# The entry half of the feed-forward layers: x rewritten in place as the normalized input, and 2 columns fewer per matmul

## The chip, the cores and the metric

The kernel runs on one core of a Trainium2 chip. The metric is the device time of one execution in microseconds (us). The engines are named as in the profile: PE is the matmul engine (TensorE), PEld its loading of weights, DVE is VectorE, ACT is ScalarE, POOL is GpSimd, SP is SyncE, which issues most of the DMAs.

## The reference

Two layers of an encoder are run over 576 tokens (512 of a prompt and 64 of a sample, which have different modulation vectors). Each layer has two feed-forward blocks around a mixer:

```
h += 1/2 * gate1 * RMSNorm(SwiGLU(mod1(RMSNorm(h))))
x  = mod2(RMSNorm(h)); ... ; h += gate2 * RMSNorm(m @ W_out)
h += 1/2 * gate3 * RMSNorm(SwiGLU(mod3(RMSNorm(h))))

def pre_mod(h, g_pre, shift, scale):
    return rmsnorm(h, g_pre) * (1 + scale[:, None, :]) + shift[:, None, :]
def swiglu(x, w1, w2):
    g, u = jnp.split(x @ w1, 2, axis=-1)
    return (jax.nn.silu(g) * u) @ w2
```

The model width is 1024, the inner width of the feed-forward blocks is 2752, and all values are fp32.

## The kernel before

**Tiling.** Activations lie transposed, with 128 features on the partitions and the 576 tokens along the free axis, so x is 8 tiles (KD) of 128x576. A weight chunk is 128x1024: the 8 tiles that take all of x to one block of 128 outputs. The first matrix of a feed-forward block has 43 chunks, which alternate between g (even) and u (odd), and chunk 42 holds the remaining 64 + 64 outputs. There are four such phases: "f1a" and "f1b" of layer 0 and of layer 1. They are called here 0a, 0b, 1a and 1b.

**Three products for one.** Every operand is split into a high and a low fp32r part, and `split_tile` (the matmul at L769) makes hi\*hi, lo\*hi and hi\*lo, each in two halves of the tokens (b = 0 and 1). A tile is thus 6 matmuls and a chunk 48. The weights are split on the way: SP loads a chunk into `w_raw` (5 slots), ACT casts it to `w_hi` (`split_hi`, L1296), DVE subtracts to get `w_lo` (`split_lo`, L1715), and PE waits in `chunk_ready` for the `w_lo` of a chunk. Both engines take the chunks strictly in order, wherever `split_hi()` and `split_lo()` stand in their programs. When a phase begins, chunks 0 to 4 are through or on their way; in `ffn_up` the next calls make chunks 5, 6, 7, and so on.

**The norm after the matmul.** `x_hi`/`x_lo` hold h\*(1+scale)\*gain, without the factor r2 = 1/rms and without the shift. Two extra moving columns (`moving(1)`, 290 columns in place of 288) carry the shift vectors of prompt and sample through the same weights. DVE then reads each chunk's result with `take` (L1792, L1793): it multiplies by `r2` and copies the two shift sums to `c_col`; the shift is added as the bias of the Silu on ACT (L1323) and in the product of g and u on DVE (L1765). ACT casts the product to `hid_hi` (L1327) and DVE makes `hid_lo` (L1770) for the second matrix.

**Order.** The result of a chunk lies in one of four pairs of PSUM banks. Chunks 0, 1 and 2 use pairs 0, 1 and 2 and are taken without r2 by ACT (`first_raw`, L1344), as r2 is being made meanwhile. Then even chunks use pair 0 and odd ones pair 1, one after the other (`whole_chunk`), each waiting in `pair_free` until the chunk before it in its pair was taken. On ACT and DVE `ffn_up` is a loop over i, the block of chunks 2i and 2i+1. Between these steps DVE works through "ada" units (L1729, two passes and two reads of the accumulator each), parts of the modulation vectors for later stages, out of two slots that POOL refills (L2432); their results pass through banks 5 and 6, which belong to pairs 2 and 3. `f1_units` says how many units stand in block i: 3 in most.

Of the kernel before, what the change touches and what calls it, by code (L numbers as in the profile page):

```python
# [8 lines left out]
ACT = mybir.ActivationFunctionType  # L9
# [65 lines left out]
          ("f1b", F1_CHUNKS), ("f2b", KF)]  # L75
TRI_PAIRS = [0, 1, 2] + [(g + T + 1) % 2 for T in range(1, NP + 1) for g in range(3)]
GROUPS = [("f1a", KF - 1, KF - 1), ("f2a", KD // 2, KD // 2), ("tri", TRI_PAIRS.count(0), TRI_PAIRS.count(1)), ("uc", 1, 1),
          ("gate", 3 * KD, 3 * KD), ("out", 4, 3), ("f1b", KF - 1, KF - 1), ("f2b", KD // 2, KD // 2)]
# [75 lines left out]
def chunk(l, ph, i):  # L154
    return l * CHUNK_N + CHUNK_AT[ph][0] + i
# [216 lines left out]
def build_program(nc, ins, outs):  # L372
# [64 lines left out]

    rms = sb("rms", [P, 3, TOK], at=big + 2 * TOK * 4)
# [122 lines left out]
    hid_ready = S("hid_ready", 2 * KF)  # L561
# [29 lines left out]
    sil_ready = S("sil_ready", 2 * KF)  # L591
    g_scaled = S("g_scaled", 4)
# [164 lines left out]
    def _(pe):  # L757
# [1922 lines left out]
```

## Time and profile before

| | |
|---|---|
| median of 3 runs | 2693.69 us (2693.58 to 2693.96) |
| the profiled execution | 2693.93 us, of which the span is 2691.9 us |
| PE | busy 2658.2 us, 99% of the span, 20698 matmuls |
| DVE | busy 1635.2 us, 61% |
| ACT | busy 962.4 us, 36% |
| POOL | busy 199.4 us, 7% |

The span reaches from the first to the last instruction of the profiled execution, and its own time has 2 us more around it. Rows of a time line give the start, the duration and the number of instructions merged into one row, and in brackets the idle time of the engine just before and what ended it. The duration of a matmul holds its pipeline, so it is longer than the distance to the next one.

### The profile page before, as it was taken

How to read it: one execution, taken by the hardware profiler on the slowest of the kernel's cores; microseconds unless marked ns; L12 is line 12 of the kernel's file. 1: busy time of each engine (PE TensorE's matmuls, PEld its weight loads, DVE VectorE, ACT ScalarE, POOL GpSimd, SP SyncE). 2: the span in 40 equal slices, each digit the busy share in tenths (PEclk: the TensorE clock that was granted, in tenths of full speed). 3: DMA queues.
4: the chain of work that ended last, by engine and by line, in shares of the span. 5: the costliest groups of instructions: out<-in, count | busy, mean ns of one | idle time of the engine just before them, and what ended most of it. 6: DMA issues, size and time to landing. Idle time of an engine off the chain costs nothing.

```text
span 2691.9 us, 49072 instructions
## 1 busy us (share of the span) xinstructions
PE 2658.2 (99%) x20698; PEld 2575.7 (96%) x20698; DVE 1635.2 (61%) x3542; ACT 962.4 (36%) x1792; POOL 199.4 (7%) x371
## 2 busy tenths in 40 slices
PE   7999999999999999999999999999999999999997
PEld 6999999888999999999999999998889999999997
DVE  4677666765655577776577776276655445555523
ACT  4222324444422442232252222255452236322321
POOL 0111110110000001111101111001100000000000
PEclk9999999999999999999999999999999999999999
DMA  6344453343333224445424445234332222333321
GB/s 260 126 145 139 158 177 112 123 130 107 95 111 109 87 95 153 135 144 163 136 88 152 137 159 157 88 101 141 119 104 81 85 83 75 98 108 104 95 81 65
DMA packets 92987, 324.79 MB, mean 121 GB/s; under 512 B 13980, under 2 KB 17628, under 8 KB 92064
## 3 DMA queue, kind: packets, MB, share of 16 engines
q1 hardware_dynamic: 62512, 221.72, 25.9%
q0 software_dynamic: 30256, 99.93, 11.2%
q8 instruction: 164, 2.69, 0.4%
q14 instruction: 55, 0.45, 0.0%
HBM read 310.70 MB, written 11.55 MB: 120 GB/s over the span
## 4 chain that ended last, share of the span: by engine, by line
PE 97%; DVE 1%; DMA 0%; issue 0%; ACT 0%; DVEq 0%; SPq 0%; ACTq 0%
PE ps L769 90%; PE ps L1131 2%; PE ps L1179 1%; PE ps L1155 1%; PE ps L778 1%; DMA ada_first<-in_ada_first 0%; PE ps L1148 0%; PE ps L823 0%; DVE prob L2242 0%; PE ps L909 0%; PE ps L1192 0%; DVE next L1792 0%; PE ps L807 0%; PE ps L832 0%; PE ps L1055 0%
## 5 line engine op out<-in xcount | busy, mean ns | idle before, releaser
L769 PE MATMUL ps<-x_hi,w_hi 128*128 128x288 f32 (+1 forms) x4224 | 940.1, 298 | 2.4 <-DVE x_lo L1883 1.5
L769 PE MATMUL ps<-x_lo,w_hi 128*128 128x288 f32 (+1 forms) x4224 | 934.2, 297 | 0.0
L769 PE MATMUL ps<-x_hi,w_lo 128*128 128x288 f32 (+1 forms) x4224 | 927.1, 295 | 0.0
L769 PEld LDWEIGHTS ps<-x_hi,w_hi 128*128 128x128 f32 x4224 | 685.2, 189 | 14.2 <-issue 8.0
L769 PEld LDWEIGHTS ps<-x_hi,w_lo 128*128 128x128 f32 x4224 | 688.3, 189 | 0.0
L769 PEld LDWEIGHTS ps<-x_lo,w_hi 128*128 128x128 f32 x4224 | 687.8, 189 | 0.3
L1715 DVE TENSOR_TENSOR w_lo<-w_raw,w_hi 128x1024 fp32r<-128x1024 f32 x384 | 467.7, 1222 | 158.8 <-ACT w_hi L1296 156.7
L1296 ACT CAST w_hi<-w_raw 128x1024 fp32r<-128x1024 f32 x384 | 391.5, 1048 | 69.4 <-DMA w_raw<-in_f 68.7
L769 PE MATMUL ps<-hid_hi,w_hi 128*128 128x288 f32 x1344 | 301.3, 295 | 0.0
L769 PE MATMUL ps<-hid_hi,w_lo 128*128 128x288 f32 x1344 | 299.8, 294 | 0.0
L769 PE MATMUL ps<-hid_lo,w_hi 128*128 128x288 f32 x1344 | 299.8, 294 | 0.0
L1729 DVE CUSTOM_DVE_ANT_0 ps<-ada_w,c_half,ada_all 128x512 f32<-128x512 f32 x256 | 193.5, 756 | 113.9 <-DMA ada_w<-in_ada 113.5
L2432 POOL DMA_DIRECT2D ada_w<-in_ada x256 | 137.7, 538 | 1639.2 <-DVE ada_all L1729 1634.9
L769 PEld LDWEIGHTS ps<-hid_hi,w_hi 128*128 128x128 f32 x1344 | 220.0, 188 | 0.2
L769 PEld LDWEIGHTS ps<-hid_lo,w_hi 128*128 128x128 f32 x1344 | 219.6, 188 | 0.2
L1327 ACT CAST hid_hi<-hid 128x576 fp32r<-128x576 f32 x84 | 56.6, 674 | 453.5 <-DVE hid L1765 453.5
L769 PEld LDWEIGHTS ps<-hid_hi,w_lo 128*128 128x128 f32 x1344 | 217.5, 188 | 0.0
L1729 DVE CUSTOM_DVE_ANT_0 ada_w<-ada_w,c_half,ada_all 128x512 f32<-128x512 f32 x256 | 191.3, 747 | 0.0
L1323 ACT ACTIVATE sil<-sil,z 128x512 f32<-128x512 f32 (+1 forms) x168 | 80.9, 529 | 249.8 <-DVE z L1793 249.6
L1792 DVE TENSOR_TENSOR hid<-ps,r 128x576 f32<-128x576 f32 x80 | 60.6, 757 | 152.9 <-PE ps L769 152.9
L1808 DVE TENSOR_TENSOR acc_y<-acc_y,sq 128x576 f32<-128x576 f32 (+1 forms) x51 | 32.9, 645 | 177.2 <-ACT sq L1367 151.4
L1367 ACT ACTIVATE sq<-ps 128x576 f32<-128x576 f32 x38 | 24.8, 654 | 299.0 <-PE ps L778 266.0
(243 smaller groups left out, 2440.9 us busy)
## 6 DMA issues: line engine op xcount, KB each, us to landing
w_raw<-in_f SPq DMA_DIRECT2D x260, 512.0 KB, 3.7
ada_w<-in_ada POOLq DMA_DIRECT2D x256, 256.0 KB, 4.0
w_raw<-in_gate SPq DMA_DIRECT2D x64, 512.0 KB, 3.7
w_raw<-in_tri SPq DMA_DIRECT2D x40, 512.0 KB, 3.7
ada_first<-in_ada_first SPq DMA_DIRECT2D x4, 2048.0 KB, 20.6
w_raw<-in_wout SPq DMA_DIRECT2D x16, 512.0 KB, 3.6
c_half<-c_scratch POOLq DMA_DIRECT2D x11, 512.0 KB, 5.8
decay_p<-f_prompt POOLq DMA_DIRECT2D x8, 512.0 KB, 4.4
```

Source lines behind the costliest of these rows:

```text
L769: r = mm(ps[:, 2 * out + b, 0:width], w, xx[:, cols(b)], start=first and n == 0, stop=last and n == 2)
L778: r = mm(ps[:, 2 * out + b, 0:HALF], w[:, s, t * P:(t + 1) * P], hid_hi[:, k, columns(b)], start=False, stop=w is w_lo)
L1131: r = mm(out, q_st[rows, i * P:i * P + m], k, start=True, stop=True)
L1155: r = turn_in(out, prob[0:m, place(u), b * P:b * P + w], const[0:m, IDENT, 0:m])
L1296: copy(w_hi[:, c % SLOTS, :], w_in[:, c % SLOTS, :]).then_inc(hi_ready.sem, 1)
L1323: r = A(sil[:, i, part], sil[:, i, part], ACT.Silu, bias=c_col[:, 2 * (i % 2), g:g + 1])
L1327: copy(hid_hi[:, i, :], hid[:, i, :]).then_inc(prod_hi.sem, 1)
L1715: V.tensor_tensor(w_lo[:, s, :], w_in[:, s, :], w_hi[:, s, :], ALU.subtract).then_inc(lo_ready.sem, 1)
L1729: r = V.tensor_tensor_reduce(out, ada_w[:, u % 2, :], c_half[:, g, :], 1.0, so_far, ALU.mult, ALU.add, so_far)
L1792: V.tensor_tensor(two(dst), pair[p], two(r2[:, :]), ALU.mult)
L1808: V.tensor_tensor(total, total, more, ALU.add).then_inc(y_added.sem, 1)
L2432: nc.gpsimd.dma_start(dst, src).then_inc(signal.sem, 16)
```

## The change

In all four first-matrix phases, chunks 0 to 5 stay as they are. Chunks 6 and 7 are run together, tile by tile, into pairs 2 and 3 (`chunk_pair`), and still read the old x. After block 1, DVE makes h\*r2 in four steps of two tiles (`h_times_r2`) and ACT turns each tile into the full normalized and shifted input `x_full` (`full_of_h`, two ACTIVATEs each). When chunks 6 and 7 have read tile k of the old x, ACT overwrites `x_hi` of this tile (`high_of_full`) and DVE `x_lo` (`low_of_full`). Chunks 8 and 9 are again run together, into pairs 0 and 1, each tile after its `x_full_ready`, and from there on all matmuls have 288 columns. From block 4 on, ACT applies the Silu straight from PSUM and DVE multiplies u from PSUM with it: there is no scaling by r2, no shift and no copy of shift sums. The ada units move to blocks 5 to 10 and 12 to 17, up to 4 in each.

```diff
@@ -73,9 +73,11 @@
 assert 2 * TAIL == P
 CHUNKS = [("f1a", F1_CHUNKS), ("f2a", KF), ("tri", 3 * (NP + 1)), ("uc", 2), ("gate", 4 * KD), ("out", KD),
           ("f1b", F1_CHUNKS), ("f2b", KF)]
+NORMED = 4
+F1_GROUPS = KF - 2
 TRI_PAIRS = [0, 1, 2] + [(g + T + 1) % 2 for T in range(1, NP + 1) for g in range(3)]
-GROUPS = [("f1a", KF - 1, KF - 1), ("f2a", KD // 2, KD // 2), ("tri", TRI_PAIRS.count(0), TRI_PAIRS.count(1)), ("uc", 1, 1),
-          ("gate", 3 * KD, 3 * KD), ("out", 4, 3), ("f1b", KF - 1, KF - 1), ("f2b", KD // 2, KD // 2)]
+GROUPS = [("f1a", F1_GROUPS, F1_GROUPS), ("f2a", KD // 2, KD // 2), ("tri", TRI_PAIRS.count(0), TRI_PAIRS.count(1)), ("uc", 1, 1),
+          ("gate", 3 * KD, 3 * KD), ("out", 4, 3), ("f1b", F1_GROUPS, F1_GROUPS), ("f2b", KD // 2, KD // 2)]
 
 N_MODS = DEPTH * N_MOD
 
@@ -123,7 +125,13 @@
 
 def f1_units(l, ab, i):
 
-    return 0 if i in (2, 11, KF - 2) else 1 if (l, ab) == (1, "b") else 3
+    n = 2 if (l, ab) == (1, "b") else 4
+    return n if 5 <= i < 11 or 12 <= i < 18 else 0
+
+
+def f1_group(p, i):
+
+    return i - 2 + p if i >= NORMED else i // 2 if p == 0 else i
 
 
 def f2_units(l, ab):
@@ -435,6 +443,7 @@
     sil = sb("sil", [P, KF, TOK], at=big)
     hid = sb("hid", [P, KF - 1, TOK], at=big + KF * TOK * 4)
 
+    x_full = sb("x_full", [P, KD, TOK], at=big + 6 * TOK * 4)
     rms = sb("rms", [P, 3, TOK], at=big + 2 * TOK * 4)
     sq_h = sb("sq_h", [P, KD, TOK], at=big + 5 * TOK * 4)
 
...
+    sil_ready = S("sil_ready", 2 * (NORMED + 1))
+    g_scaled = S("g_scaled", 6)
     tail_made = S("tail_made", 2)
     tail_in = S("tail_in", 2, step=32)
     q_scaled = S("q_scaled", NP)
...
@@ -798,6 +812,22 @@
                 r = split_tile(p, c, t, hi[:, t, :], lo[:, t, :], cols, t == 0, t == KD - 1)
             r.then_inc(chunk_done.sem, 1)
 
+        def chunk_pair(l, ph, i, pairs, cols, ab):
+
+            c = chunk(l, ph, 2 * i)
+            chunk_ready(c)
+            chunk_ready(c + 1)
+            for k in range(KD):
+                n = (ab == "b") * KD + k
+                if i == NORMED:
+                    pe.wait_ge(x_full_ready.sem, x_full_ready.done(l, n))
+                for s in (0, 1):
+                    r = split_tile(pairs[s], c + s, k, x_hi[:, k, :], x_lo[:, k, :], cols, k == 0, k == KD - 1)
+                    if k == KD - 1:
+                        r.then_inc(chunk_done.sem, 1)
+                if i < NORMED and k < KD - 1:
+                    r.then_inc(x_read.sem, 1)
+
         def x_half(l, ph, s, k, b):
 
             return split_tile(s, chunk(l, ph, s), k, x_hi[:, k, :], x_lo[:, k, :], moving, k == 0, k == KD - 1, (b,))
@@ -925,13 +955,18 @@
             whole_chunk(l, ph, 3, 1, 1, x_hi, x_lo, moving,
                         gate=(lambda t: t == BANDS_AT and sum_of_h(*((l, n - 1) if n else (l - 1, 2))))
                         if l or n else None)
-            for i in range(2, KF):
-                whole_chunk(l, ph, 2 * i, 0, i - 1, x_hi, x_lo, moving)
+            whole_chunk(l, ph, 4, 0, f1_group(0, 2), x_hi, x_lo, moving)
+            whole_chunk(l, ph, 5, 1, f1_group(1, 2), x_hi, x_lo, moving)
+            if l or n:
+                pe.wait_ge(norm_made.sem, norm_made.done(*((l, n - 1) if n else (l - 1, 2))))
+            chunk_pair(l, ph, 3, (2, 3), moving, ab)
+            for p in (0, 1):
+                pair_free(l, ph, p, f1_group(p, NORMED))
+            chunk_pair(l, ph, NORMED, (0, 1), split_columns, ab)
+            for i in range(NORMED + 1, KF):
+                whole_chunk(l, ph, 2 * i, 0, f1_group(0, i), x_hi, x_lo, split_columns)
                 if i < KF - 1:
-                    whole_chunk(l, ph, 2 * i + 1, 1, i, x_hi, x_lo, moving)
-                if i == 2 and (l or n):
-
-                    pe.wait_ge(norm_made.sem, norm_made.done(*((l, n - 1) if n else (l - 1, 2))))
+                    whole_chunk(l, ph, 2 * i + 1, 1, f1_group(1, i), x_hi, x_lo, split_columns)
             ph = "f2" + ab
             at = 0 if ab == "a" else KF + KD
             for o in range(KD - 1):
...
-            for i in range(KF - 1):
+            for i in range(NORMED):
                 if i == 1 and not l and ab == "a":
                     split_hi()
                 if i < 2:
-                    act.wait_ge(g_scaled.sem, g_scaled.done(l, (ab == "b") * 2 + i))
+                    act.wait_ge(g_scaled.sem, g_scaled.done(l, first + i))
+                elif i == 2:
+                    split_hi()
+                    act.wait_ge(acc_free[0].sem, acc_free[0].done(l, GROUP_AT[ph][0] + f1_group(0, i)))
                 else:
-                    split_hi()
-                    act.wait_ge(acc_free[0].sem, acc_free[0].done(l, GROUP_AT[ph][0] + i - 1))
+                    for k in range(KD):
+                        high_of_full(l, ab, k)
+                        if k in (2, 5):
+                            split_hi()
+                    act.wait_ge(g_scaled.sem, g_scaled.done(l, first + 2))
                 for g, part in ((0, slice(0, SEQ)), (1, slice(SEQ, TOK))):
                     r = A(sil[:, i, part], sil[:, i, part], ACT.Silu, bias=c_col[:, 2 * (i % 2), g:g + 1])
                 r.then_inc(sil_ready.sem, 1)
 
                 act.wait_ge(hid_ready.sem, hid_ready.done(l, mine + i))
                 copy(hid_hi[:, i, :], hid[:, i, :]).then_inc(prod_hi.sem, 1)
-                if i > 1:
+                if i == 1:
+                    for k in range(KD):
+                        full_of_h(l, ab, k)
+                if i == 2:
                     split_hi()
+            for i in range(NORMED, KF - 1):
+                split_hi()
+                act.wait_ge(chunk_done.sem, chunk_done.done(0, chunk(l, ph, 2 * i)))
+                A(two(sil[:, i, :]), pair[0], ACT.Silu).then_inc(acc_free[0].sem, 1)
+                split_hi()
+                act.wait_ge(acc_free[1].sem, acc_free[1].done(l, GROUP_AT[ph][1] + f1_group(1, i)))
+                copy(hid_hi[:, i, :], hid[:, i, :]).then_inc(prod_hi.sem, 1)
             split_hi()
             act.wait_ge(tail_in.sem, tail_in.done(l, ab == "b"))
             A(tail_gu[0:TAIL, :], tail_gu[0:TAIL, :], ACT.Silu)
             A(tail_ug[TAIL:P, :], tail_ug[TAIL:P, :], ACT.Silu).then_inc(sil_ready.sem, 1)
-            act.wait_ge(hid_ready.sem, hid_ready.done(l, mine + KF - 1))
+            act.wait_ge(hid_ready.sem, hid_ready.done(l, mine + NORMED))
             copy(hid_hi[:, KF - 1, :], tail_hid[:, :]).then_inc(prod_hi.sem, 1)
+
+        def full_of_h(l, ab, k):
+
+            n = 0 if ab == "a" else 2
+            act.wait_ge(x_times_r2.sem, x_times_r2.done(l, (n // 2 * KD + k) // 2))
+            for g, part in ((0, slice(0, SEQ)), (1, slice(SEQ, TOK))):
+                r = A(x_full[:, k, part], x_full[:, k, part], ACT.Identity, scale=pre_scale[:, n, k, g:g + 1],
+                      bias=shifts(l, n)[:, k, g:g + 1])
+            r.then_inc(x_full_made.sem, 1)
+
+        def high_of_full(l, ab, k):
+
+            n = (ab == "b") * KD + k
+            act.wait_ge(x_full_made.sem, x_full_made.done(l, n))
+            if k < KD - 1:
+                act.wait_ge(x_read.sem, x_read.done(l, (ab == "b") * (KD - 1) + k))
+            else:
+                chunk_over(l, "f1" + ab, 7)
+            copy(halves_of(x_hi[:, k, :]), two(x_full[:, k, :])).then_inc(x_full_high.sem, 1)
 
         def first_raw(l, ab):
 
...
@@ -1752,13 +1822,21 @@
                     take(hid[:, 1, :], 1, 3).then_inc(acc_free[1].sem, 1)
                 elif i == 1:
                     split_lo()
+                    h_times_r2(0)
+                elif i == 2:
+                    dve.wait_ge(chunk_done.sem, chunk_done.done(0, chunk(l, ph, 4)))
+                    take(sil[:, i, :], 0, 0).then_inc(acc_free[0].sem, 1)
+                    split_lo()
+                    dve.wait_ge(chunk_done.sem, chunk_done.done(0, chunk(l, ph, 5)))
+                    take(hid[:, i, :], 1, 1).then_inc(acc_free[1].sem, 1)
                 else:
-                    dve.wait_ge(chunk_done.sem, chunk_done.done(0, chunk(l, ph, 2 * i)))
-                    take(sil[:, i, :], 0, 2 * (i % 2)).then_inc(acc_free[0].sem, 1)
-                    split_lo()
-                    ada(l, ph, f1_units(l, ab, i) // 2)
-                    dve.wait_ge(chunk_done.sem, chunk_done.done(0, chunk(l, ph, 2 * i + 1)))
-                    take(hid[:, i, :], 1, 2 * (i % 2) + 1).then_inc(acc_free[1].sem, 1)
+                    for k in range(KD):
+                        low_of_full(l, ab, k)
+                        if k in (2, 5):
+                            split_lo()
+                    dve.wait_ge(chunk_done.sem, chunk_done.done(0, chunk(l, ph, 7)))
+                    take(sil[:, i, :], 2, 2).then_inc(g_scaled.sem, 1)
+                    take(hid[:, i, :], 3, 3)
                 dve.drain()
                 dve.wait_ge(sil_ready.sem, sil_ready.done(l, mine + i))
                 for g, part in ((0, slice(0, SEQ)), (1, slice(SEQ, TOK))):
...
@@ -1766,26 +1844,48 @@
                                                scalar=c_col[:, 2 * (i % 2) + 1, g:g + 1], in1=sil[:, i, part],
                                                op0=ALU.add, op1=ALU.mult)
                 r.then_inc(hid_ready.sem, 1)
+                if i == 1:
+                    for k in range(2, KD, 2):
+                        h_times_r2(k)
                 dve.wait_ge(prod_hi.sem, prod_hi.done(l, at + i))
                 V.tensor_tensor(hid_lo[:, i, :], hid[:, i, :], hid_hi[:, i, :], ALU.subtract
                                 ).then_inc(prod_lo.sem, 1)
-                if i > 1:
+                if i == 2:
                     split_lo()
-                    ada(l, ph, f1_units(l, ab, i) - f1_units(l, ab, i) // 2)
+            for i in range(NORMED, KF - 1):
+                split_lo()
+                ada(l, ph, f1_units(l, ab, i) // 2)
+                dve.wait_ge(chunk_done.sem, chunk_done.done(0, chunk(l, ph, 2 * i + 1)))
+                dve.wait_ge(acc_free[0].sem, acc_free[0].done(l, GROUP_AT[ph][0] + f1_group(0, i)))
+                V.tensor_tensor(two(hid[:, i, :]), pair[1], two(sil[:, i, :]), ALU.mult).then_inc(acc_free[1].sem, 1)
+                split_lo()
+                dve.wait_ge(prod_hi.sem, prod_hi.done(l, at + i))
+                V.tensor_tensor(hid_lo[:, i, :], hid[:, i, :], hid_hi[:, i, :], ALU.subtract
+                                ).then_inc(prod_lo.sem, 1)
+                ada(l, ph, f1_units(l, ab, i) - f1_units(l, ab, i) // 2)
             i = KF - 1
...
             upper = hid_hi[TAIL:P, i, :]
             V.tensor_tensor(upper, tail_hid[TAIL:P, :], upper, ALU.subtract).then_inc(prod_lo.sem, 1)
+
+        def h_times_r2(k):
+
+            V.tensor_tensor(x_full[:, k:k + 2, :], h[:, k:k + 2, :], r2[:, :].rearrange("p (a n) -> p a n", a=1)
+                            .to_broadcast((P, 2, TOK)), ALU.mult).then_inc(x_times_r2.sem, 1)
+
+        def low_of_full(l, ab, k):
+
+            dve.wait_ge(x_full_high.sem, x_full_high.done(l, (ab == "b") * KD + k))
+            V.tensor_tensor(halves_of(x_lo[:, k, :]), two(x_full[:, k, :]), halves_of(x_hi[:, k, :]), ALU.subtract
+                            ).then_inc(x_full_ready.sem, 1)
 
         def take(dst, p, c):
 
```

Left out are the declarations of the changed semaphores, and the tail (chunk 42), where two small additions of the shift go. New are the semaphores `x_read`, `x_times_r2`, `x_full_made`, `x_full_high` and `x_full_ready`.

## Rows read from the trace of the kernel before

**Rows 1.** The page: its head, busy time by engine.
```profile
span 2691.9 us, 49072 instructions
...
PE 2658.2 (99%) x20698; PEld 2575.7 (96%) x20698; DVE 1635.2 (61%) x3542; ACT 962.4 (36%) x1792; POOL 199.4 (7%) x371
```

**Rows 2.** The page: the chain that ended last, shares by line.
```profile
PE ps L769 90%; PE ps L1131 2%; PE ps L1179 1%; PE ps L1155 1%; PE ps L778 1%; DMA ada_first<-in_ada_first 0%; PE ps L1148 0%; PE ps L823 0%; DVE prob L2242 0%; PE ps L909 0%; PE ps L1192 0%; DVE next L1792 0%; PE ps L807 0%; PE ps L832 0%; PE ps L1055 0%
```

**Rows 3.** The chain in order of time, phase 1b and after.
```profile
2282.21 270.14 PE ps L769 x2034
...
2570.02 16.59 PE ps L769 x126
...
2655.59 8.29 PE ps L769 x63
```

**Rows 4.** Time line of all engines, pair 1 being freed in 0a.
```profile
49.93 0.65 ACT L1344 COPY hid<-ps 128x576 f32<-128x576 f32 x1
...
50.72 0.37 PE L769 MATMUL ps<-x_hi,w_hi 128*128 128x288 f32 x1 [0.48 <-ACT hid L1344]
```

**Rows 5.** DVE time line, phase 1b.
```profile
2292.77 1.22 DVE L1715 TENSOR_TENSOR w_lo<-w_raw,w_hi 128x1024 fp32r<-128x1024 f32 x1
2294.08 0.95 DVE L1765 SCALAR_TENSOR_TENSOR hid<-hid,z,sil 128x512 f32<-128x512 f32 x2
...
2297.18 1.21 DVE L1715 TENSOR_TENSOR w_lo<-w_raw,w_hi 128x1024 fp32r<-128x1024 f32 x1
2299.77 0.76 DVE L1792 TENSOR_TENSOR hid<-ps,r 128x576 f32<-128x576 f32 x1 [1.38 <-PE ps L769]
...
2325.26 0.76 DVE L1792 TENSOR_TENSOR hid<-ps,r 128x576 f32<-128x576 f32 x1 [4.42 <-PE ps L769]
```

**Rows 6.** ACT time line, phase 1b.
```profile
2291.97 0.96 ACT L1323 ACTIVATE sil<-sil,z 128x512 f32<-128x512 f32 x2
2295.06 0.67 ACT L1327 CAST hid_hi<-hid 128x576 fp32r<-128x576 f32 x1 [2.13 <-DVE hid L1765]
2295.64 1.05 ACT L1296 CAST w_hi<-w_raw 128x1024 fp32r<-128x1024 f32 x1
```

**Rows 7.** DVE time line, phase 0a.
```profile
60.91 1.23 DVE L1715 TENSOR_TENSOR w_lo<-w_raw,w_hi 128x1024 fp32r<-128x1024 f32 x1 [0.19 <-ACT w_hi L1296]
...
70.11 0.76 DVE L1792 TENSOR_TENSOR hid<-ps,r 128x576 f32<-128x576 f32 x1 [3.57 <-PE ps L769]
```

**Rows 8.** Groups by line and shape, ACT.
```profile
L1371 ACT ACTIVATE z<-ps,z 128x288 f32<-128x288 f32 x48 | 23.7, 495 | 0.0
...
L1308 ACT ACT_TABLE_LOAD x3 | 3.8, 1283 | 0.1
```

**Rows 9.** Groups by line and shape, PE.
```profile
L823 PE MATMUL ps<-sq_h,const 128*32 128x288 f32 x160 | 11.8, 412 | 0.0
...
L892 PE MATMUL ps<-sq_in,const 128*32 128x288 f32 x32 | 4.1, 687 | 11.6 <-DVE sq_in L2002 11.6
```

**Rows 10.** Stretches: length, busy PE, PEld, DVE, ACT, POOL, clock, DMA share, GB/s.
```profile
20.00:23.50 3.50, 1.56 (x9) 1.13 (x9) 3.50 (x6) 3.43 (x7) 0.00 (x0) 1.00 1.01 418
23.50:24.00 0.50, 0.50 (x5) 0.50 (x4) 0.50 (x2) 0.50 (x1) 0.00 (x0) 0.85 1.01 426
24.00:24.50 0.50, 0.50 (x7) 0.22 (x9) 0.46 (x2) 0.01 (x1) 0.00 (x0) 0.50 1.06 451
27.00:27.50 0.50, 0.50 (x20) 0.44 (x12) 0.00 (x0) 0.00 (x0) 0.00 (x0) 0.73 1.00 426
```

**Rows 11.** DVE time line, ada units in 0a.
```profile
114.40 0.09 DVE L1729 DVE_READ_ACCUMULATOR2_ANT ada_all<- 128x1 f32 x1
...
118.95 0.76 DVE L1729 CUSTOM_DVE_ANT_0 ps<-ada_w,c_half,ada_all 128x512 f32<-128x512 f32 x1 [1.25 <-DMA ada_w<-in_ada]
...
121.10 0.76 DVE L1792 TENSOR_TENSOR hid<-ps,r 128x576 f32<-128x576 f32 x1 [0.72 <-PE ps L769]
```

More of the change, by code:

```diff
@@ L560, in build_program @@
     prod_lo = S("prod_lo", 2 * KF + KD)
-    hid_ready = S("hid_ready", 2 * KF)
+    hid_ready = S("hid_ready", 2 * (NORMED + 1))
+    x_read = S("x_read", 2 * (KD - 1))
+    x_times_r2 = S("x_times_r2", KD)
+    x_full_made = S("x_full_made", 2 * KD)
+    x_full_high = S("x_full_high", 2 * KD)
+    x_full_ready = S("x_full_ready", 2 * KD)
     merged = S("merged", KD)
@@ L1302, in ffn_up @@
             ph, at = "f1" + ab, (0 if ab == "a" else KF + KD)
-            mine = 0 if ab == "a" else KF
+            mine, first = (0, 0) if ab == "a" else (NORMED + 1, 3)
             if l or ab == "b":
@@ L1738, in ffn_up @@
             ph, at = "f1" + ab, (0 if ab == "a" else KF + KD)
-            mine = 0 if ab == "a" else KF
+            mine, first = (0, 0) if ab == "a" else (NORMED + 1, 3)
             if l or ab == "b":
                 norm_of_h(*((l, 1) if ab == "b" else (l - 1, 2)))
-            for i in range(KF - 1):
+            for i in range(NORMED):
                 if i == 0:
@@ L1771, in ffn_up @@
                                 ).then_inc(prod_lo.sem, 1)
-                if i > 1:
+                if i == 2:
                     split_lo()
-                    ada(l, ph, f1_units(l, ab, i) - f1_units(l, ab, i) // 2)
+            for i in range(NORMED, KF - 1):
[9 more added lines that the diff above has]
+                ada(l, ph, f1_units(l, ab, i) - f1_units(l, ab, i) // 2)
             i = KF - 1
             dve.wait_ge(chunk_done.sem, chunk_done.done(0, chunk(l, ph, 2 * i)))
-            take(tail_gu[:, :], 0, 2 * (i % 2)).then_inc(acc_free[0].sem, 1)
+            V.tensor_copy(two(tail_gu[:, :]), pair[0]).then_inc(acc_free[0].sem, 1)
             dve.drain()
-            for g, part in ((0, slice(0, SEQ)), (1, slice(SEQ, TOK))):
-                r = V.tensor_scalar(tail_gu[:, part], tail_gu[:, part], c_col[:, 2 * (i % 2), g:g + 1], None, ALU.add)
-            r.then_inc(tail_made.sem, 1)
+            dve.sem_inc(tail_made.sem, 1)
             split_lo()
             modulated_all(l, ph)
-            dve.wait_ge(sil_ready.sem, sil_ready.done(l, mine + i))
+            dve.wait_ge(sil_ready.sem, sil_ready.done(l, mine + NORMED))
             V.tensor_tensor(tail_hid[:, :], tail_gu[:, :], tail_ug[:, :], ALU.mult).then_inc(hid_ready.sem, 1)
```

2 lines of the change are left out of this document (removed).

## The prediction

> **What bounds the kernel now.** The page's busy times come first: PE is busy 99% of a span of 2691.9 us with 20698 matmuls [rows 1]. The chain that ended last says the same by line: 90% of the span is the matmul of `split_tile` at L769 [rows 2]. So a change counts only through (1) what the matmuls of L769 take and (2) what makes PE wait. The chain in order of time shows how little it waits today: in phase 1b one unbroken piece of 270.14 us with 2034 matmuls [rows 3]. The time lines of DVE and ACT at a phase's start then show how early their results are ready.
>
> **1. Two columns fewer.** The price of the two columns is the difference of two distances. With 288 and 290 columns in turn, DVE takes the result of chunk 5 at 2299.77 and of chunk 9 at 2325.26, each time after waiting for PE: 25.49 us for 4 chunks of 48 matmuls, 132.76 ns each [rows 5]. With 288 columns alone, in the second matrix, five outputs of 130 matmuls (126 of L769 and 4 of the tail) lie between 2570.02 and 2655.59: 131.65 ns [rows 3]. The difference is 1.11 ns a matmul. It applies to chunks 8 to 42, 35 x 48 = 1680 matmuls in each of 4 phases: 6720 x 1.11 ns = **-7.5 us**. The bound from below: 2 of 288 columns, if the time went with the columns alone, are 131.65 x 2/288 = 0.91 ns in every second matmul, 3.1 us in all. I take 7.5, as both rows are the same line in long runs. The Trainium skill ("TensorE: Matmul & The Clock Gate", Back-to-back issue gap) puts the distance of matmuls at the columns over the clock plus 2.5 ns; that is 122.5 ns for 288 columns, which this trace does not bear out, and two columns would be 0.83 ns, 2.8 us in all.
>
> **2. Chunk 7's weights come late.** This is the large term. `chunk_pair` for 6 and 7 waits in `chunk_ready` for both before its first matmul. Chunk 7 is the weight split that both engines make at the head of block 2. Before, ACT casts it at 2295.64 [rows 6] and DVE finishes at 2297.18 + 1.21 = 2298.4 [rows 5]. PE wants chunk 6 right after chunk 5, at about 2299.6 (DVE, which waits for chunk 5's end, sees it at 2299.77), and chunk 7 only 6.4 us later. After the change, ACT's program has the 8 tiles of `full_of_h` behind block 1 and ahead of this cast. Step by step in phase 1b:
> - DVE splits chunk 6 at 2292.77, and the product of block 1 starts 1.31 later, at 2294.08 [rows 5]. Between them now stands the first `h_times_r2`, 2 x 576 elements. A DVE pass of 576 lasts 0.76 and one of 1024 lasts 1.21 [rows 5], so 1152 take 1.35, some 1.3 from start to start. The product moves to 2295.4.
> - ACT's cast of it starts 0.98 after the product does and hands over 0.58 later [rows 5, 6]: `full_of_h` begins at 2296.95. DVE's other three `h_times_r2`, 1.3 each, run from 2296.3 and are done by 2300.2, ahead of the tiles that need them.
> - One tile is two ACTIVATEs of 512 and 64 elements. The Silu of the same two shapes lasts 0.96 [rows 6], and rows on ACT overlap by 0.09 (0.67 lasting, 0.58 apart), so 0.87. An Identity with a scale at L1371 has 0.495 for 288 [rows 8], of the same order. 8 x 0.87 = 7.0: ACT is free at 2303.9.
> - The cast of chunk 7 lasts 1.05 [rows 6], its subtraction 1.21 [rows 5] (DVE took chunk 4 by 2301.6 and waits there): 2306.2. A release reached PE 0.14 after its end (ACT copy 49.93 + 0.65, PE 50.72) [rows 4]: PE starts at 2306.3.
>
> So PE stands 6.7 us. Phases 0b and 1a repeat these rows at the same distances, so three times 6.7. In 0a chunk 6 is split at 60.91 and chunk 5 ends at 70.11, a distance of 9.2 in place of 7.0 [rows 5, 7]: 6.7 - 2.2 = 4.5. Sum **+24.6 us**. Nothing hides it: PE has no other work queued between chunks 5 and 6. The bounds: 0.8 to 1.0 a tile moves each stall by -0.6 or +1.0, giving 22 to 29.
>
> Identity's table is a further cost that no row shows. A table load lasts 1.28 [rows 8]; before the first tile of each phase it would add 5.1 us in all. I take nothing, since L1371 applies Identity under another set of tables without a load of its own. The Trainium skill ("ScalarE: Activation LUTs", Table sets: the hidden batching unit) has identity in every set, which would also make it nothing.
>
> **3. Behind the stall.** I looked for what is late next. Pair 6/7 lasts 12.75 us, 1.59 a tile. ACT's `high_of_full` (0.58 each) and DVE's `low_of_full` (0.67) follow PE tile by tile; the splits of chunks 8, 9 and 10 fit between and are done over 5 us before they are needed; tile 7 is free at the pair's end and ready about 1.5 us later, while pair 8/9 wants it after 7/8 of its 12.6 us. No wait there. The new hand-over of pair 0 does show. Chunk 8 ends only 6 matmuls (0.8 us) ahead of chunk 9, then ACT reads 576 elements from PSUM (0.65, as at L1344) with some 0.15 ahead and 0.14 behind it, so chunk 10 waits about 0.2: **+0.8 us** in four phases (0 to 1.6).
>
> DVE loses the takes, copies of shifts and half-products, but gets 4 ada units in 12 blocks in place of 3 in 16. A slot was refilled 118.95 - 114.49 = 4.5 us after its last read [rows 11]; units last 1.35. Four units with two slots then take 3.4 + 1.8 of waiting beyond a split + 2.7, and with both splits, the multiply and the subtraction (1.2, 1.2, 0.75, 0.75 and short waits) about 11.5 of a block's 12.6 us. Results would have to be 5 us late before PE notices, so nothing.
>
> **4. The clock.** At the start PE was busy 1.56 of the 3.5 us from 20.0 to 23.5; the granted clock then fell from 1.00 over 0.85 to 0.50 (1.2 GHz) and rose within the half microsecond that shows 0.73, up to 27.5 [rows 10]: 3.4 us at the low level. After 11.6 us without work the first matmuls lasted 687 ns, against 412 for the same shape later [rows 9]. The new stalls have no PE work at all for 4.6 to 6.7 us, so I expect a fall in each. 3.4 us at half speed lose 1.7 where PE has work; some of it will lie inside the stall. I take 1.2 a phase, **+4.8 us**, between 0 and 6.8. The Trainium skill ("TensorE: Matmul & The Clock Gate", Part 1) says that idling throttles the array to half rate until it is busy again; by that rule, and the trace agrees, each stall is followed by a slow stretch.
>
> **The sum** is -7.5 + 24.6 + 0.8 + 4.8 = +22.7 us against the profiled execution's 2693.93, so 2716.6; the median of the runs is 0.24 lower, hence 2716.4, rounded to 2716.
>
> **The rivals.**
> - Stalls, but the clock stays up. For it: no row shows a full stop of this length in mid-kernel. Against it: rows 9 and 10. 2693.7 - 7.5 + 24.6 + 0.8 = 2711.6.
> - No stall (the other side). This is so if the tiles on ACT overlap or DVE and ACT reach chunk 7 in time. The point is plain: the cast must start by 2297.2, so 8 tiles may take 0.3 us in place of 7.0. In its favour stands only that I read an order out of the program. 2693.7 - 7.5 + 0.8 = 2687.0, faster by 0.25%.
> - The ada units make DVE the bound. With a refill 1 us slower than the 4.5 above, a block would lose about a microsecond in 12 blocks of three phases once the 5 us in hand are used up: 7 x 3 = 21 us more, 2737. Against it: the rows have refills of 4.5 throughout.
>
> **How the numbers follow.** Stalls with the clock falling 0.70, stalls with the clock up 0.17, no stall 0.05, ada 0.03, the rest (stalls of half the size, 2699 to 2706) 0.05. The first has its own range of 2709 (22 of stalls, nothing of clock) to 2725 (3.1 saved, 27 of stalls, 6.8 of clock). With the second the range is 2706 to 2725. No case but the third is below the line of 0.2% (5.4 us), about what a measurement of this kernel can tell from no change: faster 0.04, same 0.03, slower 0.93.
>
> **What would show it.** In the changed trace PE should have one gap of 6 to 7 us in each of three phases and one of 4 to 5 us in 0a, ended by the `w_lo` split of chunk 7 on DVE, which itself waited for ACT's cast behind 16 ACTIVATEs; the clock at 0.50 behind each; distances of 131.65 ns from chunk 8 on; a wait of 0.2 us for ACT's Silu at chunk 10; and none for x tiles. The prediction is wrong if ACT's tiles are much quicker, if the gap ends with another engine, or if 288 columns don't bring 131.65 ns here.

## The result and the profile after

The changed kernel takes 2722.64 us (median of 4 runs, 2722.16 to 2723.44), the kernel before 2693.64 us beside it (4 runs): a ratio of 1.0112 with a 95% interval of 1.0100 to 1.0125. It is slower by 29.0 us, where 22.7 were forecast, and inside the range of 2706 to 2725. One execution of the run e5_no_gap below, the profiled one, took 5246.21 us where its others took 2685, and stands in no median here.

The page of the changed kernel, head and busy time, against [rows 1]:

```profile
span 2720.4 us, 48824 instructions
...
PE 2656.7 (98%) x20698; PEld 2572.7 (95%) x20698; DVE 1546.7 (57%) x3238; ACT 994.7 (37%) x1820; POOL 199.4 (7%) x371
```

PE does its 20698 matmuls in about the same busy time, but in a span 28.5 us longer: the time went into waits. The waits of PE (engine and line, whom it waited for, us in total, times, longest):

```profile
PE ps L783 <- DVE w_lo L1785: 29.9, 5, 7.9
```

L783 is `split_tile` (L769 before) and L1785 is `split_lo`. Four of the five waits, 29.5 us together, are those at chunk 6; the fifth, 0.5 us, is in the start-up, and the kernel before has one of 0.4 us there too. The chain in order of time through the start of phase 1b tells the rest; before, it was one piece of matmuls there [rows 3]:

```profile
2313.24 1.14 DVEq L1840
2314.38 1.27 DVE x_full L1881
...
2315.74 0.96 DVE hid L1843 x2
...
2316.72 0.68 ACT hid_hi L1368
2317.40 8.30 ACT x_full L1393 x16
2325.70 0.94 ACT w_hi L1331
...
2326.67 1.24 DVE w_lo L1785
2327.90 0.14 issue
2328.04 27.34 PE ps L783 x192
...
2355.42 4.58 PE ps L783 x33
```

It is the chain forecast, link by link: the first h\*r2 (L1881), the product of block 1 (L1843), ACT's cast of it (L1368), sixteen ACTIVATEs for x_full (L1393), the cast (L1331) and the subtraction (L1785) of chunk 7, then 192 matmuls of the chunks 6 to 9. One link is longer than forecast, 8.30 us in place of 7.0. DVE's and ACT's time lines beside [rows 5, 6]:

```profile
2314.30 1.35 DVE L1881 TENSOR_TENSOR x_full<-h,r 128x1152 f32<-128x1152 f32 x1
2315.74 0.94 DVE L1843 SCALAR_TENSOR_TENSOR hid<-hid,z,sil 128x512 f32<-128x512 f32 x2
2316.61 3.89 DVE L1881 TENSOR_TENSOR x_full<-h,r 128x1152 f32<-128x1152 f32 x3
...
2321.08 0.75 DVE L1892 TENSOR_TENSOR sil<-ps,r 128x576 f32<-128x576 f32 x1
...
2326.67 1.23 DVE L1785 TENSOR_TENSOR w_lo<-w_raw,w_hi 128x1024 fp32r<-128x1024 f32 x1 [4.77 <-ACT w_hi L1331]
```

```profile
2316.72 0.68 ACT L1368 CAST hid_hi<-hid 128x576 fp32r<-128x576 f32 x1 [3.40 <-DVE hid L1843]
2317.30 8.40 ACT L1393 ACTIVATE x_full<-x_full,ada_all,z 128x512 f32<-128x512 f32 x16
2325.61 1.03 ACT L1331 CAST w_hi<-w_raw 128x1024 fp32r<-128x1024 f32 x1
```

DVE has read the result of chunk 4 by 2321.8 and then sits idle for 4.77 us until ACT's cast. PE's first matmuls after the wait, and the first ones after chunk 9:

```profile
2328.04 0.82 PE L783 MATMUL ps<-x_hi,w_hi 128*128 128x288 f32 x2 [7.91 <-DVE w_lo L1785]
2328.66 0.68 PE L783 MATMUL ps<-x_lo,w_hi 128*128 128x290 f32 x2
2329.14 0.69 PE L783 MATMUL ps<-x_hi,w_lo 128*128 128x288 f32 x2
```

```profile
2354.95 0.43 PE L783 MATMUL ps<-x_hi,w_lo 128*128 128x288 f32 x2
2355.42 0.50 PE L783 MATMUL ps<-x_hi,w_hi 128*128 128x288 f32 x2
```

PE was idle for 7.91 us; 6 to 7 were forecast. Two matmuls then take 0.48 us (2328.66 to 2329.14) in place of 0.26. At chunk 10 the two matmuls ahead of the new chunk take 0.47 in place of 0.26: the hand-over of pair 0, 0.2 us as forecast. After that the matmuls of 288 columns lie 131.67 ns apart (the 1215 from 2371.5 to 2531.5), where it was 132.77 in the same stretch of the kernel before. The granted clock in half microseconds, the third number from the right (for columns see [rows 10]):

```profile
72.00:72.50 0.50, 0.00 (x0) 0.00 (x0) 0.00 (x0) 0.50 (x2) 0.00 (x0) 0.82 0.33 131
74.50:75.00 0.50, 0.03 (x1) 0.06 (x1) 0.50 (x2) 0.00 (x0) 0.00 (x0) 0.50 0.00 0
...
79.00:79.50 0.50, 0.50 (x5) 0.50 (x5) 0.50 (x2) 0.00 (x0) 0.00 (x0) 0.86 0.00 0
```

```profile
987.00:987.50 0.50, 0.00 (x0) 0.00 (x0) 0.00 (x0) 0.50 (x2) 0.00 (x0) 0.59 0.00 0
...
993.50:994.00 0.50, 0.50 (x4) 0.50 (x4) 0.50 (x1) 0.48 (x1) 0.00 (x0) 0.59 0.00 0
1410.00:1410.50 0.50, 0.00 (x0) 0.00 (x0) 0.00 (x0) 0.50 (x1) 0.00 (x0) 0.84 0.00 0
1417.00:1417.50 0.50, 0.50 (x5) 0.50 (x4) 0.45 (x1) 0.50 (x1) 0.00 (x0) 0.83 0.00 0
2325.00:2325.50 0.50, 0.00 (x0) 0.00 (x0) 0.00 (x0) 0.50 (x2) 0.00 (x0) 0.61 0.00 0
2331.50:2332.00 0.50, 0.50 (x5) 0.50 (x4) 0.50 (x1) 0.50 (x1) 0.00 (x0) 0.56 0.00 0
```

In every phase the clock fell to 0.50, which is 1.2 GHz, while PE stood still, and stayed there for about 6.8 us. PE worked at that level for the last 4.2 us of it in 0a, 3.9 in 0b, 2.9 in 1a and 3.9 in 1b.

### The profile page after: what moved, and what is told of

Its sections match the earlier page's. It is cut to its first block, busy times and chain, and to the rows that moved or that the text cites. A ratio compares the mean times of both kernels' runs of the same rounds, so it can differ in the third digit from the quotient of the medians.

```text
span 2720.4 us, 48824 instructions
## 1 busy us (share of the span) xinstructions
PE 2656.7 (98%) x20698; PEld 2572.7 (95%) x20698; DVE 1546.7 (57%) x3238; ACT 994.7 (37%) x1820; POOL 199.4 (7%) x371
## 4 chain that ended last, share of the span: by engine, by line
PE 94%; DVE 3%; ACT 2%; DMA 0%; DVEq 0%; issue 0%; SPq 0%; ACTq 0%
PE ps L783 86%; PE ps L1166 2%; ACT x_full L1393 1%; PE ps L1214 1%; PE ps L1190 1%; PE ps L792 1%; DMA ada_first<-in_ada_first 0%; DVE w_lo L1785 0%; PE ps L1183 0%; PE ps L853 0%; DVE prob L2342 0%; PE ps L1227 0%; PE ps L939 0%; DVE hid L1843 0%; DVE next L1892 0%
## 5 line engine op out<-in xcount | busy, mean ns | idle before, releaser
L783 PE MATMUL ps<-x_hi,w_hi 128*128 128x288 f32 (+1 forms) x4224 | 943.4, 299 | 32.1 <-DVE w_lo L1785 29.9
L783 PE MATMUL ps<-x_lo,w_hi 128*128 128x288 f32 (+1 forms) x4224 | 928.5, 296 | 0.0
L783 PE MATMUL ps<-x_hi,w_lo 128*128 128x288 f32 (+1 forms) x4224 | 925.7, 295 | 0.0
L783 PEld LDWEIGHTS ps<-x_hi,w_hi 128*128 128x128 f32 x4224 | 684.3, 189 | 45.8 <-issue 32.4
L783 PEld LDWEIGHTS ps<-x_lo,w_hi 128*128 128x128 f32 x4224 | 687.2, 189 | 0.3
L783 PEld LDWEIGHTS ps<-x_hi,w_lo 128*128 128x128 f32 x4224 | 686.7, 189 | 0.0
L1785 DVE TENSOR_TENSOR w_lo<-w_raw,w_hi 128x1024 fp32r<-128x1024 f32 x384 | 467.8, 1222 | 179.2 <-ACT w_hi L1331 175.8
L1331 ACT CAST w_hi<-w_raw 128x1024 fp32r<-128x1024 f32 x384 | 398.5, 1047 | 80.8 <-DMA w_raw<-in_f 79.2
L783 PE MATMUL ps<-hid_hi,w_hi 128*128 128x288 f32 x1344 | 301.1, 295 | 0.0
L783 PE MATMUL ps<-hid_lo,w_hi 128*128 128x288 f32 x1344 | 299.3, 293 | 0.0
L783 PE MATMUL ps<-hid_hi,w_lo 128*128 128x288 f32 x1344 | 299.0, 294 | 0.0
L1860 DVE TENSOR_TENSOR hid<-ps,sil 128x576 f32<-128x576 f32 x68 | 51.5, 758 | 314.1 <-PE ps L783 314.0
L783 PEld LDWEIGHTS ps<-hid_hi,w_hi 128*128 128x128 f32 x1344 | 219.8, 188 | 0.2
L783 PEld LDWEIGHTS ps<-hid_lo,w_hi 128*128 128x128 f32 x1344 | 219.4, 188 | 0.2
L783 PEld LDWEIGHTS ps<-hid_hi,w_lo 128*128 128x128 f32 x1344 | 217.2, 187 | 0.0
L1380 ACT CAST hid_hi<-hid 128x576 fp32r<-128x576 f32 x68 | 45.9, 676 | 353.6 <-DVE hid L1860 353.6
L1377 ACT ACTIVATE sil<-ps 128x576 f32<-128x576 f32 x68 | 44.3, 651 | 268.7 <-PE ps L783 268.7
```

The lines of the kernel that those rows point to most:

```text
L783: r = mm(ps[:, 2 * out + b, 0:width], w, xx[:, cols(b)], start=first and n == 0, stop=last and n == 2)
L1331: copy(w_hi[:, c % SLOTS, :], w_in[:, c % SLOTS, :]).then_inc(hi_ready.sem, 1)
L1377: A(two(sil[:, i, :]), pair[0], ACT.Silu).then_inc(acc_free[0].sem, 1)
L1380: copy(hid_hi[:, i, :], hid[:, i, :]).then_inc(prod_hi.sem, 1)
L1785: V.tensor_tensor(w_lo[:, s, :], w_in[:, s, :], w_hi[:, s, :], ALU.subtract).then_inc(lo_ready.sem, 1)
L1860: V.tensor_tensor(two(hid[:, i, :]), pair[1], two(sil[:, i, :]), ALU.mult).then_inc(acc_free[1].sem, 1)
```

## The experiments

The phase length used below runs from the first matmul of the sum of h at chunk 3 (in 0a: from the end of its wait for pair 1) to the first matmul of the second matrix. It leaves out what the second matrix, the mixer and the start-up do. All in us:

| kernel | 0a | 0b | 1a | 1b | PE's waits for a split in the four phases |
|---|---|---|---|---|---|
| before | 255.01 | 254.31 | 254.31 | 254.31 | none |
| changed | 261.28 | 262.64 | 262.15 | 262.59 | 5.74, 7.91, 7.91, 7.91 |
| e1_act_first | 254.52 | 258.75 | 256.00 | 256.00 | 0.87, 3.04, 3.05, 3.04 |
| e2_both_first | 253.40 | 253.94 | 253.96 | 253.94 | 0, 0.99, 0.99, 0.99 |
| e3_columns_only | 253.13 | 252.45 | 252.45 | 252.44 | none |
| e4_scale_only | 259.41 | 261.89 | 261.75 | 262.09 | 4.26, 6.42, 6.43, 6.42 |
| e6_early_pair0 | 253.13 | 252.44 | 252.45 | 252.45 | none |
| e8_no_gap_again | 253.41 | 252.72 | 252.72 | 252.71 | none |

The end points in 1b, as an example of how the table is read, of the kernel before and of e3_columns_only (2535.38 - 2281.07, 2525.18 - 2272.74):

```profile
2281.07 0.89 PE L832 MATMUL ps<-sq_h,const 128*128 128x288 f32 x3
```

```profile
2535.38 0.43 PE L769 MATMUL ps<-hid_hi,w_hi 128*128 128x288 f32 x2
```

```profile
2272.74 0.65 PE L832 MATMUL ps<-sq_h,const 128*128 128x288 f32 x2
```

```profile
2525.18 0.42 PE L769 MATMUL ps<-hid_hi,w_hi 128*128 128x288 f32 x2
```

**e1_act_first.** Only ACT's order is changed.

```diff
                 elif i == 2:
-                    split_hi()
                     act.wait_ge(acc_free[0].sem, acc_free[0].done(l, GROUP_AT[ph][0] + f1_group(0, i)))
...
                 r.then_inc(sil_ready.sem, 1)
+                if i == 1:
+                    split_hi()
```

> The changed kernel, with ACT's cast of chunk 7 ahead of the eight x tiles (behind the Silu of block 1, where ACT waits anyway); DVE's program is unchanged. Theory (the stall is ACT's queue): DVE's subtraction of chunk 7 then stands behind the four products h*r2, hid_lo and the take of chunk 4, which end at 2321.9 in phase 1b, so chunk 7 is ready at about 2323.2 in place of 2327.9. PE's gap at chunk 6 falls by 4.7 us in each phase, to 3.2 in 0b, 1a and 1b and 1.0 in 0a: 4 x 4.7 = 19 us less, 2703.6. If the shorter gaps leave the clock at its full level, 7 us less again, 2697. Rival (the rewriting of x or DVE sets the gap): within 2 us of 2722.6.

Measured: 2700.75 us (8 runs, 2699.08 to 2701.85), 1.0028 of before (1.0017 to 1.0038), between the two times expected, with and without falls of the clock. Moving one cast, with all work kept, takes 21.9 us off the changed kernel. The waits are near what the theory gives for DVE's queue: 3.04 for 3.2 in three phases, and 0.87 for 1.0 in 0a. The clock did something not foreseen: PE's first matmuls behind the two equal waits of 0b and 1a, and the clock there (0.50 in the first stretch, 1.00 in the last):

```profile
978.20 0.82 PE L783 MATMUL ps<-x_hi,w_hi 128*128 128x288 f32 x2 [3.04 <-DVE w_lo L1786]
978.82 0.69 PE L783 MATMUL ps<-x_lo,w_hi 128*128 128x290 f32 x2
```

```profile
1398.63 0.50 PE L783 MATMUL ps<-x_hi,w_hi 128*128 128x288 f32 x2 [3.05 <-DVE w_lo L1786]
1398.96 0.43 PE L783 MATMUL ps<-x_lo,w_hi 128*128 128x290 f32 x2
```

```profile
977.00:977.50 0.50, 0.00 (x0) 0.00 (x0) 0.50 (x1) 0.50 (x2) 0.00 (x0) 0.97 0.75 287
978.00:984.00 6.00, 5.80 (x24) 5.83 (x25) 2.43 (x6) 4.99 (x10) 0.00 (x0) 0.50 0.03 10
984.00:984.50 0.50, 0.50 (x5) 0.50 (x4) 0.31 (x2) 0.50 (x2) 0.00 (x0) 0.70 0.00 0
1397.00:1404.00 7.00, 5.37 (x40) 5.41 (x41) 3.42 (x8) 5.99 (x13) 0.00 (x0) 1.00 0.17 64
```

In 0b it fell and in 1a and 1b it did not, and the phases differ by 258.75 - 256.00 = 2.75 us. So a wait of 3.04 us cost its length alone in two phases, and nearly as much again in the third, where the clock fell shortly before its end and PE worked at the low level for 6 us. Why it fell in 0b and not in 1a and 1b is not shown.

**e2_both_first.** As e1, with DVE's subtraction moved as well.

```diff
                     take(sil[:, i, :], 0, 0).then_inc(acc_free[0].sem, 1)
-                    split_lo()
...
                 if i == 1:
+                    split_lo()
                     for k in range(2, KD, 2):
                         h_times_r2(k)
```

> As e1_act_first, and DVE's subtraction of chunk 7 also stands ahead of the last three products h*r2. Theory: chunk 7 is ready at 2317.9 in phase 1b, before PE ends chunk 5 at 2320.0, so there is no gap at chunk 6 and no fall of the clock: 2722.6 - 30 - 7 = 2686. The rewriting of x is now 8 us nearer to PE: chunk 9's split, behind the third tile on both engines, should be some 1 us late for the pair 8 and 9, at most 4 us in all: 2686 to 2690. Rival (the stall only moves): PE waits at chunks 8 and 9 for as long as it did at 6, and the time stays above 2710.

Measured: 2689.52 us (10 runs), 0.9989 of before (0.9979 to 0.9998), where 2686 to 2690 were expected. The wait at chunk 6 is gone, and what is late next is chunk 9's split, at chunk 8, by 1 us in the three phases; the clock stays up. The rival, that the stall only moves, falls.

PE's waits for `split_lo`, three of 0.99 and one in the start-up:

```profile
PE ps L783 <- DVE w_lo L1786: 3.4, 4, 1.0
```

**e3_columns_only.** The kernel before, without the shift columns from chunk 8 on; it leaves the shift of these chunks out of the result.

```diff
-                whole_chunk(l, ph, 2 * i, 0, i - 1, x_hi, x_lo, moving)
+                cols = moving if i < 4 else split_columns
+                whole_chunk(l, ph, 2 * i, 0, i - 1, x_hi, x_lo, cols)
                 if i < KF - 1:
-                    whole_chunk(l, ph, 2 * i + 1, 1, i, x_hi, x_lo, moving)
+                    whole_chunk(l, ph, 2 * i + 1, 1, i, x_hi, x_lo, cols)
```

> The kernel before, with 288 columns from chunk 8 on and nothing else changed; the shift sums of these chunks are left out (the copies of them stay and read what chunks 3 and 4 and the ones before left). It prices the two columns alone. By the distances of the trace before (1.11 ns a matmul, 6720 matmuls) 7.5 us less, 2686.2; by the balance of the changed kernel's phases (2.1 us a phase) 8.5 less, 2685.2. Rival (time in proportion to the columns): 3.1 us less, 2690.6.

Measured: 2683.49 us (5 runs), 0.9967 (0.9954 to 0.9980). The phases are 1.88, 1.86, 1.86 and 1.87 us shorter, 7.5 in all and 1.11 ns a matmul: the price read from the distances, and neither the 8.5 nor the 3.1 us. The medians differ by 9.4; the other 1.9 us lie outside the phases (see below the table of the next section), and the 18 executions of the kernel before beside it range over 2.7 (2691.22 to 2693.96).

**e4_scale_only** and **e7_bias_only** take one of the two per-partition operands off the sixteen ACTIVATEs: e4 leaves out the shift, e7 (diff not shown) the scale.

```diff
-                r = A(x_full[:, k, part], x_full[:, k, part], ACT.Identity, scale=pre_scale[:, n, k, g:g + 1],
-                      bias=shifts(l, n)[:, k, g:g + 1])
+                r = A(x_full[:, k, part], x_full[:, k, part], ACT.Copy, scale=pre_scale[:, n, k, g:g + 1])
```

> The changed kernel, with the scale but without the shift as bias in the ACTIVATEs that make x_full; the shift is left out of chunks 8 to 42. Its ACTIVATEs took 0.80 and 0.43 us there, the Silu of the same shapes, which has a bias and no scale, 0.72 and 0.33. Theory (a second operand per partition costs some 0.09 an instruction): the sixteen instructions take 7.0 us in place of 8.4, the gap of PE is 1.4 us shorter in each phase, 5.6 in all, 2717. Rival (the price is the Identity itself or reading x_full): no difference, 2722.6.

> The changed kernel, with the shift but without the scale in the ACTIVATEs that make x_full; the factor (1 + scale) * gain is left out of chunks 8 to 42. Theory (each instruction with two operands per partition pays some 0.09 us more than with one, whichever it is): 0.71 and 0.33 us as in e4_scale_only, a gap of 6.4 us. Rival (Identity is slower than Copy): 0.80 and 0.43 us as in the changed kernel, a gap of 7.9 us.

Measured: 2718.46 us (4 runs) and 2719.09 us (one run). The group of these instructions in the changed kernel, in e4 and in e7:

```profile
L1393 ACT ACTIVATE x_full<-x_full,ada_all,z 128x512 f32<-128x512 f32 x32 | 25.6, 801 | 0.0
...
L1393 ACT ACTIVATE x_full<-x_full,ada_all,z 128x64 f32<-128x64 f32 x32 | 13.6, 425 | 0.0
```

```profile
L1393 ACT ACTIVATE x_full<-x_full,z 128x512 f32<-128x512 f32 x32 | 22.7, 708 | 0.0
...
L1393 ACT ACTIVATE x_full<-x_full,z 128x64 f32<-128x64 f32 x32 | 10.6, 332 | 0.0
```

```profile
L1393 ACT ACTIVATE x_full<-x_full,ada_all 128x512 f32<-128x512 f32 x32 | 22.7, 708 | 0.0
...
L1393 ACT ACTIVATE x_full<-x_full,ada_all 128x64 f32<-128x64 f32 x32 | 10.6, 332 | 0.0
```

Copy with a scale and Identity with a bias last the same, 708 and 332 ns, and both operands together 801 and 425: 93 ns for the second one, at both lengths. Copy or Identity makes no difference. The waits are 1.5 us shorter, where 1.4 were expected. The time fell by 4.2 us in place of 5.6, and the phases by 1.87, 0.75, 0.40 and 0.50 us. The clock is the reason: PE resumes earlier and then works at the low level for longer in three of the four phases, 5.6, 5.2 and 6.0 us in 0b, 1a and 1b in place of 3.9, 2.9 and 3.9. The four pieces of 192 matmuls behind the waits take 27.12, 28.13, 27.98 and 28.32 us, 9.0 more than at full clock where the changed kernel's take 6.6 more; the waits give 5.9 back and the clock takes 2.4 of it. In 1b the low level lasted from 2319.6 to 2329.9, 10 us in place of 6.8. In 0a it lasted only 3.4 us, and began at 73.7, half a microsecond after the wait of 4.26 had ended at 73.19.

**e5_no_gap**, **e6_early_pair0** and **e8_no_gap_again.** All splits are moved ahead of their need. On ACT, against e2_both_first:

```diff
                     for k in range(KD):
                         high_of_full(l, ab, k)
-                        if k in (2, 5):
+                        if k == 5:
                             split_hi()
...
-                if i == 1:
+                if i in (1, 2):
                     split_hi()
...
                     for k in range(KD):
                         full_of_h(l, ab, k)
-                if i == 2:
-                    split_hi()
+                        if k == 3:
+                            split_hi()
```

On DVE, `split_lo()` follows also behind the `take` of chunk 4 and only one among the x_lo tiles. e6 also changes the order of the last four tiles of the pair 8 and 9 to chunk 8, chunk 8, chunk 9, chunk 9; this diff is not shown.

> All splits moved ahead of their need: as e2_both_first, and chunk 8's cast stands in the middle of the x tiles on ACT (its subtraction behind the take of chunk 4), chunk 9's behind the Silu of block 2. Theory: no wait for weights is left in any phase; against e2_both_first the 1.1 us at chunk 8 in 0b, 1a and 1b go, 3.4 us less, 2686. Against the kernel before this leaves the columns' 7.5 less and 0.2 a phase at chunk 10 more, -6.7 us. Rival (the x tiles come late now that PE is not held up): PE waits for x_lo at chunks 8 and 9, and the time stays at 2689.5 or rises.

> As e5_no_gap, with the last two tiles of chunk 8 run ahead of the last two of chunk 9, so that chunk 8 ends 12 matmuls before chunk 9 in place of 6. Theory (chunk 10 waits for ACT's Silu to free pair 0): the 0.2 us at chunk 10 go in four phases, 0.8 us less than e5_no_gap, which only the time line can tell, not the time. Rival (the 0.2 us are the start of a new group): the same 0.2 us.

> e5_no_gap once more, for its time lines. Theory: no wait of PE for a split in the four phases, each phase 1.7 us shorter than before, and 0.2 us at chunk 10, which e6_early_pair0 does not have.

Measured: e5 2685.09 us (7 runs), 0.9972 of before (0.9961 to 0.9983); e6 2683.59 us (5 runs), 0.9967 (0.9954 to 0.9979), against 2692.54 us of before beside them. e8 is e5's kernel once more, 2684.00 us (one run, before 2690.82 beside it), and its time lines are used here. PE waits in it for no split and no rewritten x tile in the four phases, which are each 1.6 us shorter than before; so the rival of e5, that the x tiles come late, falls too. The chain in 0a, from the first matmul of chunk 3 past chunk 10, in e8 and then in e6:

```profile
49.67 44.75 PE ps L783 x336
94.41 0.04 issue
94.45 15.64 PE ps L783 x117
```

```profile
50.20 59.88 PE ps L783 x451
```

In e8 there is the short break at chunk 10 and in e6 none, and each of the four phases differs by 0.26 to 0.28 us, which only the time lines tell; the rival of e6, that a new group costs this anyway, falls. e6's phases are those of e3_columns_only to 0.01 us: all the work of rewriting x is hidden there, and all that the two columns are worth is kept.

**e9_gap_at_half** repeats e2.

> e2_both_first once more. With gaps of 1 us in three phases the clock should stay at its full level throughout, as in its first trace; a fall in any of them would say that gaps far below 3 us can cost a slow stretch too.

Measured: 2687.52 us (one run, before 2690.82 beside it), waits of 0.99 in three phases and the clock at 1.00 through all four, as in e2_both_first.

## Why the prediction was right, and where its sizes were off

| term | forecast | measured |
|---|---|---|
| two columns, 6720 matmuls | -7.5 | -7.5 (e3_columns_only) |
| PE's stop at chunk 6 | +24.6 | +30.1 |
| hand-over of pair 0 at chunk 10 | +0.8 | +0.8 to 1.1 |
| clock behind the stop | +4.8 | +6.6 |
| sum | +22.7 | +30.0 to 30.3; the four phases together +30.7, the medians +29.0 |

The measured stop is 5.90 and three times 8.07: the idle time of the rows (5.74, 7.91) and what the first matmul comes late beside the usual distance. The clock's 6.6 is the four pieces of 192 matmuls (27.51, 27.39, 26.92 and 27.34) less four times the 25.63 that the same piece took in 0a of e1_act_first at full clock. The four phases add up to 1.7 us more than the medians moved. By the two traces, the changed kernel starts chunk 3 of 0a 0.84 us earlier (49.88 against 50.72) and takes 1.0 us less from the end of phase 1a to the start of 1b (651.6 against 652.6). The trace of the kernel before is the slowest of the ten in both: they range from 49.41 to 50.72 and from 651.2 to 652.6. The two traces of one kernel, e2_both_first and e9_gap_at_half, differ by 1.3 us in the first stretch, and e3_columns_only, whose edit touches neither, is 1.4 us shorter than before in the second. So neither this 1.7 nor the 1.9 of e3_columns_only can be put down to the change; what makes these stretches scatter is not shown.

**1, the columns.** Right, and the pricing by distances within one line held to 0.1 us. The proportional bound (3.1) is refuted for this stream of 288 columns with a weight load each. So is the 2.8 by the Trainium skill ("TensorE: Matmul & The Clock Gate", Back-to-back issue gap); but that section gives its formula for an isolated matmul and says itself that a stream of weight loads and matmuls is spaced otherwise, which the prediction left out.

**2, chunk 7.** The mechanism, its place, its six links and its size relative to 0a were right. The step mis-sized is "8 x 0.87 = 7.0": a tile took 1.04, above even the 1.0 of the bound, so that the term's 30.1 lies above its stated 22 to 29 and the waits, 7.91 and 5.74, above the "6 to 7" and "4 to 5" named as signs. I took the Silu's duration, which has one operand per partition, where the new instructions have two. The nearest row in elements was not the nearest in operands. The difference, 1.4 us in each phase, is the whole error of this term. e4_scale_only and e7_bias_only show the price, 93 ns, and 16 of them are 1.5 us in each phase. The Trainium skill ("ScalarE: Activation LUTs", What ACT_TABLE_LOAD costs) states about 93 ns for each such operand, and the trace agrees to the nanosecond. The sixteen instructions run back to back in 8.40 us, which leaves no room for a table load: Identity needs none here.

**3, behind the stall.** Right: PE waits for no rewritten x tile in any of the eight traces of kernels that rewrite x, 0.2 us at chunk 10, and the 4 ada units a block were hidden. That nothing else was late was true only with the stop in place: once it is gone, chunk 9 is late by 1 us (e2_both_first). A stop hides the next one.

**4, the clock.** A fall in each phase came, with 1.65 us a phase in place of 1.2, near the upper bound of 1.7, since the low level lasted about twice as long as in [rows 10], 6.8 us for 3.4. By the rule of the Trainium skill ("TensorE: Matmul & The Clock Gate", Part 1), that idling halves the rate until the array is busy again, all four had to fall, and the trace agrees. For waits of 3.04 us this case shows both outcomes (e1_act_first). That the term stayed within its bounds, 0 to 6.8, was in part luck: in e4_scale_only, whose waits are 1.5 us shorter, the clock cost 9.0 in the four phases. The bound took the 3.4 us of [rows 10] for the length of the low level, and the traces show 3.4, 6.8 and 10.2.

**The range.** Its upper end, 2725, was added up with 27 us of stalls where the same text bounds them by 29, and its lower end, 2706, has no sum behind it. The measured 2722.64 lies inside, though the stop came out above its bound and the clock near its own, because the upper end had taken the columns at their least, 3.1 us, and they brought 7.5.

**The rivals.** That the clock stays up fell with the rows of the clock. That there is no stop fell with the waits, and e1 and e2 showed by moving nothing but the splits that it was the order of the queue. That the ada units bound DVE found no wait.

## What to carry to other kernels

When work is added to an engine's program, look at what already stands behind it in that program, not only at whether the engine has free time: ACT was busy 37% of the span of the changed kernel and still held PE up for 8 us, by one cast of 1 us placed behind 8 us of new work. Splits and loads for the next chunks go ahead of, or into the middle of, a long block of less urgent work; once that was done, the same change gained 7.5 us in the four phases, 9.0 by the medians, where it had lost 29 (e6_early_pair0). And after removing a wait, look for the next one, which it had covered.

## What was not expected of the hardware

- Two columns more in every second matmul of 288 cost 1.11 ns a matmul (e3_columns_only), 2.2 ns for the wider one, 2.4 times their share of its 131.65 ns.
- A second operand per partition on an ACTIVATE costs 93 ns at 512 elements (801 against 708) and at 64 (425 against 332), whether it is the scale or the bias (e4_scale_only, e7_bias_only).
- A wait of 3.04 us brought the clock down in one of three phases of one execution and not in the others (e1_act_first). Waits of 0.99 never did in two executions (e2_both_first, e9_gap_at_half). Waits of 4.26 to 7.91 did each time (the changed kernel, e4_scale_only, e7_bias_only).
- A shorter wait did not always cost less: behind the waits of 6.42 in e4_scale_only PE worked at the low level for 5.2 to 6.0 us, behind those of 7.91 in the changed kernel for 2.9 to 3.9. The low level lasted 3.4, 6.8 or 10.2 us, and what decides between them is not shown.
